# VectorE's order of work inside one attention head: each combination moved up behind its row maximum

## The chip, the cores and the metric

The kernel runs on one core of a Trainium2 chip. The metric is the device time of one launch in microseconds (us); lower is better. A core has five engines with a queue each, which runs in order: TensorE (PE, with its weight loads as PEld), VectorE (DVE), ScalarE (ACT), GpSimd (POOL) and SyncE (SP, which here only issues DMAs). The engines wait for each other on semaphores alone.

## The reference

One step of a streaming encoder layer on 640 tokens (512 of a prompt, 8 streams of 16): a token mixer of two branches, then a mixture of experts, then a final norm. The change touches the token mixer alone. There, per head h of 8:

```
q, k, v, xr, gr = projections of the normed tokens by w_in        # 128 columns each per head
p1, p2 = softmax(q1 k1^T), softmax(q2 k2^T)                        # two maps, chunk-causal for the prompt
attn   = rmsnorm((p1 - lam * p2) @ v)
xc     = conv_b + sum_j xpad[j:j+t] * conv_w[j]                    # causal convolution, width 4
r, i   = sigmoid(xc @ w_ra + b), sigmoid(xc @ w_ri + b)
a      = exp(-8 r softplus(-lambda)); h_t = a_t h_(t-1) + sqrt(1 - a_t^2) (i xc)_t    # recurrence (scan)
y      = h * gelu(gr)
```

The streams attend to 256 cached keys as well.

## The kernel before, in words

The kernel has stages, one `nc.Block()` each. Stage 2 is a loop over heads: head 0 stands by itself, heads 1 to 6 are three turns of a loop of two bodies, head 7 stands by itself. In the profiled execution heads 1 to 6 lie in 128 to 475 us, head 0 before them from about 70 us, and head 7 behind them up to 524 us. Every order in it is written out by hand; nothing is planned by a program. Each engine has its own `body(S)`.

**PE, head h** (L657 on): transposes of the cached keys, the scores of the streams, then this head's projections `xr0`, `xr1` (for the convolution) and `gr0`, `gr1`, and between them the projections of the NEXT head: `kv0` to `kv4` (keys and values of five token tiles), `q0`, `q1`. Among these stand the four prompt tiles qt = 0 to 3 of the attention: `scores(qt)` (L653), `turn_weights(qt)` (transposes of the combined maps, L633), `values(qt)` (L642). Order behind `xr1`: scores 0, kv0, streams' values (L710), kv1, kv2, turn_weights 0, scores 1, gr0, values 0, turn_weights 1, scores 2, gr1, values 1, kv3, turn_weights 2, scores 3, kv4, then the four gate products `ra0 ra1 ri0 ri1` of the recurrence (L735, which wait for `conv_done`), values 2, q0, q1, turn_weights 3, transposes of the keys, values 3. The heads 0 and 7 lack parts: head 0 has no recurrence of a head before to finish on DVE, head 7 has no next head to project.

**The ring of three banks.** All projections and gate products of a head (18 `UNITS`) share three PSUM banks in turn: unit n may start when unit n-3 has been copied out (`S.free`, L424 on). So `gr0` waits for the copy of `kv0`, `ra1` for that of `kv3`, `ri0` for that of `kv4`, and `ri1` for the tanh that reads `ra0`. The copies of kv and xr are on DVE (L891, L922, L932), those of q, gr, the keys and the four tanh (L834) on ACT.

**ACT, head h** (in order): exp 0 of the streams, the tail of the head before (four activations), exp 1, ..., the copies of gr0 and gr1, exp 4, then the four tanh of ra0, ra1, ri0, ri1, then q0, q1. The exponential numbered u = qt+1 (L769) waits for the row maximum of its tile; each is two activations, one per map, with the row sums.

**DVE, head h** is what the change reorders. `prompt_max(S, qt)` masks the scores and takes both maps' row maxima (L867, L860, L861), which releases exp qt+1 on ACT. `combine(S, qt)` waits for that exponential, and forms p1 - lam p2 (L881, L882, L884), which releases `turn_weights(qt)` on PE. `tail_a`, `tail_b`, `tail_c` and `norm_attention` (L443 to L482) finish the recurrence and the norm of head h-1: a reciprocal and products, the scan (L459), the gelu product, the norm. The last of them raises `rnn_done`, for which SP waits before it loads the next head's columns, cached values and the weight tile of gr. `conv` (L895 on) is the convolution, eight instructions, and raises `conv_done`.

**POOL** splits each weight tile of 512 KB into a high and a low part (L167, L170), five tiles per head, when the tile has landed and PE is done with the old one.

Of the kernel before, what the change touches and what calls it, by code (L numbers as in the profile page):

```python
# [88 lines left out]
def build(nc, A, O):  # L89
    top = ExitStack()  # L90
    with top:
# [393 lines left out]
        with nc.Block() as block:  # L485
# [369 lines left out]
            def _(dve):  # L855
# [8 lines left out]
                def prompt_max(S, qt):  # L864
                    n = (qt + 1) * P
                    dve.wait_ge(sc_done, S.h * NQ + (qt + 1))
                    chain(nc.vector.memset(pair[0:64, :, n - 64:n], -BIG))  # L867
                    row_max(S, qt + 1, n)

                def mask_new():  # L870

                    nc.vector.memset(pair[:, :, KNEW:SKEYS], -BIG).then_inc(new_masked, 1)

                def combine(S, qt):

                    u = qt + 1
                    n = (qt + 1) * P
                    dve.wait_ge(exp_done, S.h * 5 + (u + 1))
                    if qt == NQ - 1 and not S.last:
                        mask_new()  # L880
                    chain(nc.vector.reciprocal(stat[:, u, 6:8], stat[:, u, 4:6]))  # L881
                    chain(nc.vector.scalar_tensor_tensor(stat[:, u, 8:9], stat[:, u, 4:5], stat[:, u, 7:8], neglam,  # L882
                                                         ALU.mult, ALU.mult))
                    nc.vector.scalar_tensor_tensor(ebuf[u % 2][:, 0, 0:n], ebuf[u % 2][:, 1, 0:n], stat[:, u, 8:9],  # L884
                                                   ebuf[u % 2][:, 0, 0:n], ALU.mult, ALU.add).then_inc(comb_ready, 1)
# [9 lines left out]
                def conv(S):  # L895

                    cw = hcol[S.par]
                    xcs = xc[:, SEQ:TOK].rearrange("p (b q) -> p b q", q=DS)
                    for j in range(CW):
                        if j == 0:  # L900
                            nc.vector.tensor_scalar(xc[:, 0:SEQ], xpad[:, 0:SEQ], cw[:, R_CW:R_CW + 1],
                                                    cw[:, R_CB:R_CB + 1], ALU.mult, ALU.add)
                            chain(nc.vector.tensor_scalar(xcs, spad[:, :, 0:DS], cw[:, R_CW:R_CW + 1],
                                                          cw[:, R_CB:R_CB + 1], ALU.mult, ALU.add))
                            continue
                        nc.vector.scalar_tensor_tensor(xc[:, 0:SEQ], xpad[:, j:j + SEQ], cw[:, j:j + 1],
                                                       xc[:, 0:SEQ], ALU.mult, ALU.add)
                        ins = nc.vector.scalar_tensor_tensor(xcs, spad[:, :, j:j + DS], cw[:, j:j + 1],
                                                             xcs, ALU.mult, ALU.add)
                        if j < CW - 1:  # L910
                            chain(ins)
                        else:
                            ins.then_inc(conv_done, 1)

                def body(S):
                    h, par = S.h, S.par
                    base = 0 if S.first else h * (BODY_STEPS + TAIL_STEPS) - TAIL_STEPS
                    chain.at(base)
                    dve.wait_ge(ss_done, h + 1)
                    row_max(S, 0, SKEYS)  # L920
                    S.done(dve, "xr0")
                    nc.vector.tensor_copy(xpad[:, 3:3 + HALF], S.bank("xr0")[:, 0:HALF]).then_inc(pr_dve, 1)  # L922

                    dve.wait_ge(exp_done, h * 5 + 1)
                    chain(nc.vector.reciprocal(stat[:, 0, 6:8], stat[:, 0, 4:6]))
                    chain(nc.vector.tensor_scalar(stat[:, 0, 8:10], stat[:, 0, 6:8], msign, None, ALU.mult))
                    for g in range(2):
                        ins = nc.vector.tensor_scalar(selc[:, g, :], cst[:, K_SEL:K_SEL + 64],
                                                      stat[:, 0, 8 + g:9 + g], None, ALU.mult)
                    ins.then_inc(selc_ready, 1)  # L930
                    S.done(dve, "xr1")
                    nc.vector.tensor_copy(xpad[:, 3 + HALF:3 + SEQ], S.bank("xr1")[:, 0:SEQ - HALF])  # L932
                    nc.vector.tensor_copy(spad[:, :, 3:], S.bank("xr1")[:, SEQ - HALF:HALF]
                                          .rearrange("p (b q) -> p b q", q=DS)).then_inc(pr_dve, 1)
                    dve.wait_ge(col_in[par], S.i * 64 + (S.h0 // 2 * 64 + 64))
                    chain(nc.vector.tensor_copy(spad[:, :, 0:3],
                                                hcol[par][:, NCOL:NCOL + 24].rearrange("p (b w) -> p b w", w=3)))
                    prompt_max(S, 0)
                    if not S.first:
                        tail_a(dve, chain, h - 1)  # L940
                    if not S.last:
                        copy_kv(S, 0, 1 - par, h + 1)

                    dve.wait_ge(os_done, h + 1)
                    sample = ons[:, bass.ds(h, 1), :, :].rearrange("p o t c -> p (o t) c")
                    nc.vector.tensor_scalar(sample, bank[7][:, 0:2 * DV].rearrange("p (t c) -> p t c", c=DV),
                                            1.0, None, ALU.mult).then_inc(os_out, 1)
                    combine(S, 0)
                    if not S.last:
                        copy_kv(S, 1, 1 - par, h + 1)  # L950
                        copy_kv(S, 2, 1 - par, h + 1)
                    prompt_max(S, 1)
                    if not S.first:
                        tail_b(chain, h - 1, 1 - par)
                    combine(S, 1)
                    if not S.first:
                        tail_c(dve, chain, h - 1, 1 - par)
                        norm_attention(dve, chain, h - 1)
                    prompt_max(S, 2)
                    conv(S)  # L960
                    combine(S, 2)
                    if not S.last:
                        copy_kv(S, 3, 1 - par, h + 1)
                    prompt_max(S, 3)

                    nc.vector.tensor_scalar(stc[:, bass.ds(h, 1), 0:3], xpad[:, SEQ:SEQ + 3]
                                            .rearrange("p (o c) -> p o c", o=1), 1.0, None, ALU.mult)
                    nc.vector.tensor_scalar(stc[:, bass.ds(h, 1), 3:27].rearrange("p o (b w) -> p (o b) w", w=3),
                                            spad[:, :, DS:DS + 3], 1.0, None, ALU.mult)
                    if not S.last:  # L970
                        copy_kv(S, 4, 1 - par, h + 1)
                    combine(S, 3)

                    S.out(dve, "gr1")
                    chain(nc.vector.tensor_tensor(gw[:, :], gr[par][:, :], gr[par][:, :], ALU.mult))
                    chain(nc.vector.tensor_scalar(gw[:, :], gw[:, :], 0.044715, 1.0, ALU.mult, ALU.add))
                    nc.vector.tensor_tensor(gw[:, :], gw[:, :], gr[par][:, :], ALU.mult).then_inc(gcube, 1)
                    S.out(dve, "ri1")
                    nc.vector.scalar_tensor_tensor(thi[:, :], thi[:, :], 1.0, xc[:, :], ALU.add, ALU.mult)

                    dve.wait_ge(op_done, h + 1)
                    nc.vector.tensor_tensor(oraw[:, :, :], bank[7][:, :].rearrange("p (t c) -> p t c", c=DV),
                                            stat[:, 1:5, 6:7].to_broadcast([P, NQ, DV]), ALU.mult).then_inc(op_out, 1)
                    dve.wait_ge(op_out, h + 1)
                    nc.vector.tensor_tensor(ossq, sample, sample, ALU.mult)
                    chain(nc.vector.tensor_tensor(osq, oraw[:, :, :], oraw[:, :, :], ALU.mult))
                    nc.vector.tensor_reduce(oms[:, NQ:NO], ossq, AX.X, ALU.add)
                    nc.vector.tensor_reduce(oms[:, 0:NQ], osq, AX.X, ALU.add).then_inc(ms_ready, 1)
                    want = BODY_STEPS + (0 if S.first else TAIL_STEPS)
                    assert chain.n == want, (chain.n, want)  # L990
# [984 lines left out]
```

## Time and profile before

| what | value |
|---|---|
| median of 3 runs | 1348.51 us (1347.18 to 1349.4) |
| profiled execution, its own time | 1351.92 us |
| its span | 1350.1 us |
| busy: PE, DVE, ACT, POOL | 85%, 61%, 40%, 38% |
| granted TensorE clock, mean | 0.954 of full |

The span is what the profile covers; the own time is that of the same execution as the runs are timed. A row of the order of time gives an instruction's start, its duration, its engine, line, what it writes and reads, and in brackets how long its engine had been idle and what ended that. Rows that follow each other with the same line are merged with a count.

### The profile page before, as it was taken

What the parts mean: (1) busy time and instruction counts of PE and PEld (TensorE: products, weight loads), DVE (VectorE), ACT (ScalarE), POOL (GpSimd) and SP (SyncE); (2) the same over time, 40 slices, a digit from 0 to 9 for tenths busy, and PEclk for the clock granted to TensorE, in tenths of its full rate; (3) what the DMA queues carried; (4) which work ended last, traced back from release to release, by engine and by line L of the source; (5) the groups of instructions that cost most, each with busy time, mean ns of one, the idle gap of its engine ahead of it and who ended that gap; (6) DMA issues with size and microseconds to landing.
All of it is one profiled execution on the core that took longest, in us unless ns stands there. A gap on an engine that the chain in (4) does not pass through costs nothing. (4 is left out here: it accounts for less than half of the span.)

```text
span 1350.1 us, 20865 instructions
## 1 busy us (share of the span) xinstructions
PE 1152.0 (85%) x7096; PEld 980.4 (73%) x7097; DVE 824.8 (61%) x1204; ACT 542.8 (40%) x873; POOL 510.4 (38%) x267
## 2 busy tenths in 40 slices
PE   2898999899899977999899999577989989888970
PEld 1787888788788866999899845355767767776760
DVE  5436888578588767400512111448788889888765
ACT  3123342333324245111100011126767868777752
POOL 4434161433516102655566300023444444434433
PEclk9999999899999988999899999768999999999995
DMA  4362253232514201422522195024995584799936
GB/s 158 83 165 79 60 142 99 68 105 61 158 52 121 72 1 47 140 78 78 187 78 78 57 337 220 16 88 169 362 336 213 185 297 163 260 361 352 354 143 249
DMA packets 185411, 211.63 MB, mean 157 GB/s; under 512 B 12599, under 2 KB 131383, under 8 KB 185350
## 3 DMA queue, kind: packets, MB, share of 16 engines
q1 hardware_dynamic: 176422, 178.26, 40.6%
q0 software_dynamic: 4608, 16.78, 3.6%
q10 hardware_dynamic: 4320, 15.73, 2.9%
q8 instruction: 43, 0.70, 0.2%
q14 instruction: 18, 0.15, 0.0%
HBM read 184.20 MB, written 26.36 MB: 156 GB/s over the span
## 5 line engine op out<-in xcount | busy, mean ns | idle before, releaser
L1759 ACT ACTIVATE ch<-w 128x1024 fp32r<-128x1024 f32 x240 | 252.0, 1059 | 118.4 <-PE bank L1699 97.0
L1823 DVE TENSOR_TENSOR cl<-w,ch 128x1024 fp32r<-128x1024 f32 x180 | 261.1, 1497 | 41.3 <-ACT ch L1759 37.6
L1669 POOL TENSOR_TENSOR cl<-w,ch 128x1024 fp32r<-128x1024 f32 x60 | 154.2, 2570 | 229.1 <-ACT ch L1759 229.0
L167 POOL TENSOR_TENSOR wh<-raw,zcol 128x1024 fp32r<-128x1024 f32 x40 | 78.7, 1968 | 275.3 <-DMA raw<-in_w_in 194.7
L1697 PE MATMUL bank<-ch,xeh 128*128 128x512 f32 x320 | 132.9, 415 | 45.8 <-DVE cl L1823 42.7
L1698 PE MATMUL bank<-cl,xeh 128*128 128x512 f32 x320 | 127.0, 397 | 0.0
L1699 PE MATMUL bank<-ch,xel 128*128 128x512 f32 x320 | 126.9, 397 | 0.0
L591 PE MATMUL bank<-xh,wh 128*128 128x320 f32 x384 | 122.4, 319 | 0.0
L592 PE MATMUL bank<-xl,wh 128*128 128x320 f32 x384 | 119.2, 310 | 0.0
L593 PE MATMUL bank<-xh,wl 128*128 128x320 f32 x384 | 119.1, 310 | 0.0
L1697 PEld LDWEIGHTS bank<-ch,xeh 128*128 128x128 f32 x320 | 61.3, 192 | 71.8 <-DVE cl L1823 55.3
L170 POOL TENSOR_TENSOR wl<-raw,wh 128x1024 fp32r<-128x1024 f32 x40 | 97.9, 2447 | 3.1
L1117 POOL TENSOR_TENSOR w3h<-wraw,zcol 128x1024 fp32r<-128x1024 f32 x32 | 61.4, 1920 | 87.0 <-PE bank L1160 83.3
L591 PE MATMUL bank<-wh,xh 128*128 128x256 f32 x320 | 93.7, 293 | 0.0
L592 PE MATMUL bank<-wl,xh 128*128 128x256 f32 x320 | 89.9, 281 | 0.0
L593 PE MATMUL bank<-wh,xl 128*128 128x256 f32 x320 | 89.9, 281 | 0.0
L1158 PE MATMUL bank<-bh,w3h 128*128 128x320 f32 x256 | 80.3, 313 | 6.1 <-DVE bl L1240 6.1
L1121 POOL TENSOR_TENSOR w3l<-wraw,w3h 128x1024 fp32r<-128x1024 f32 x32 | 82.0, 2562 | 2.5
L769 ACT ACTIVATE ebuf<-bank,stat 128x384 f32<-128x384 f32 (+3 forms) x80 | 42.3, 534 | 98.8 <-DVE stat L861 98.8
L591 PEld LDWEIGHTS bank<-xh,wh 128*128 128x128 f32 x384 | 72.7, 189 | 10.8 <-issue 8.8
L1159 PE MATMUL bank<-bl,w3h 128*128 128x320 f32 x256 | 80.1, 313 | 0.0
L1160 PE MATMUL bank<-bh,w3l 128*128 128x320 f32 x256 | 80.0, 312 | 0.0
(277 smaller groups left out, 2686.3 us busy)
## 6 DMA issues: line engine op xcount, KB each, us to landing
w<-in_w SPq DMA_DIRECT2D x64, 1024.0 KB, 15.0
w<-in_w SPq DMA_DIRECT2D x16, 2048.0 KB, 10.1
raw<-in_w_in SPq DMA_DIRECT2D x40, 512.0 KB, 4.5
block_outputs<-yb ACTq DMA_DIRECT2D x21, 512.0 KB, 7.2
kc<-in_cache_k SPq DMA_DIRECT2D x8, 1024.0 KB, 6.7
vc<-in_cache_v SPq DMA_DIRECT2D x8, 1024.0 KB, 5.9
wraw<-in_w_in SPq DMA_DIRECT2D x16, 512.0 KB, 3.8
block_outputs<-zero ACTq DMA_DIRECT2D x9, 512.0 KB, 7.1
```

The source lines that it names most:

```text
L170: nc.gpsimd.tensor_tensor(wl[:, :, j, :], r[:, :, :], wh[:, :, j, :].bitcast(F32), ALU.subtract) \
L591: nc.tensor.matmul(out, ah, bh, start=(k == 0), stop=False)
L592: nc.tensor.matmul(out, ah, bl, start=False, stop=False)
L593: mm = nc.tensor.matmul(out, al, bh, start=False, stop=(k == len(pairs) - 1))
L1121: nc.gpsimd.tensor_tensor(w3l[j][:, :, :], wraw[j][:, :, :], w3h[j][:, :, :].bitcast(F32), ALU.subtract).then_inc(w3_split, 1)
L1158: nc.tensor.matmul(out, w3h[j][:, k, :], mh[:, k, c], start=(k == 0), stop=False)
L1669: nc.gpsimd.tensor_tensor(cl[:, c % RING5, :, :], S.raw(c), ch[:, c % RING5, :, :].bitcast(F32), ALU.subtract).then_inc(ch_low_pool, 1)
L1697: nc.tensor.matmul(out, ah, high, start=first, stop=False)
L1698: nc.tensor.matmul(out, ah, low, start=False, stop=False)
L1699: mm = nc.tensor.matmul(out, al, high, start=False, stop=end)
L1759: nc.scalar.activation(ch[:, c % RING5, :, :], S.raw(c), ACT.Copy).then_inc(ch_high, 1)
L1823: nc.vector.tensor_tensor(cl[:, c % RING5, :, :], S.raw(c), ch[:, c % RING5, :, :].bitcast(F32), ALU.subtract).then_inc(ch_low_dve, 1)
```

## The change

It moves three calls in DVE's order and touches nothing else. `combine(S, 0)` goes from behind the copy of the streams' result to directly behind `prompt_max(S, 0)`, ahead of `tail_a`. `combine(S, 1)` goes from between `tail_b` and `tail_c` to directly behind `prompt_max(S, 1)`, ahead of `tail_b`. `combine(S, 2)` goes from behind `conv` to directly behind `prompt_max(S, 2)`, ahead of `conv`. `combine(S, 3)` stays.

```diff
                     prompt_max(S, 0)
+                    combine(S, 0)
                     if not S.first:
                         tail_a(dve, chain, h - 1)
                     if not S.last:
...
                                             1.0, None, ALU.mult).then_inc(os_out, 1)
-                    combine(S, 0)
                     if not S.last:
                         copy_kv(S, 1, 1 - par, h + 1)
                         copy_kv(S, 2, 1 - par, h + 1)
                     prompt_max(S, 1)
+                    combine(S, 1)
                     if not S.first:
                         tail_b(chain, h - 1, 1 - par)
-                    combine(S, 1)
-                    if not S.first:
                         tail_c(dve, chain, h - 1, 1 - par)
                         norm_attention(dve, chain, h - 1)
                     prompt_max(S, 2)
+                    combine(S, 2)
                     conv(S)
-                    combine(S, 2)
                     if not S.last:
                         copy_kv(S, 3, 1 - par, h + 1)
                     prompt_max(S, 3)
```

## Rows read from the trace of the kernel before

**Rows 1.** The page: busy time, share of the span and instructions of each engine.
```profile
PE 1152.0 (85%) x7096; PEld 980.4 (73%) x7097; DVE 824.8 (61%) x1204; ACT 542.8 (40%) x873; POOL 510.4 (38%) x267
```
**Rows 2.** Waits of PE in 250 to 310 us (head 3): total, times, longest.
```profile
PE bank L633 <- DVE ebuf L884: 2.7, 3, 1.1
```
**Rows 3.** Waits of PE in 490 to 550 us (head 7).
```profile
PE bank L633 <- DVE ebuf L884: 9.9, 2, 7.3
...
PE bank L735 <- ACT thr L834: 1.5, 1, 1.5
```
**Rows 4.** DVE in order of time, head 3: start us, us, engine, line.
```profile
262.04 0.48 DVE L445 TENSOR_SCALAR thr<-ra 128x640 f32<-128x640 f32 x1
...
271.73 0.17 DVE L867 MEMSET bank<- 64x128 f32 x1 [0.46 <-PE bank L653]
...
272.73 0.16 DVE L456 TENSOR_TENSOR h0t<-ra,hcol 128x8 f32<-128x8 f32 x1
...
280.46 0.55 DVE L901 TENSOR_SCALAR xc<-xpad,hcol 128x512 f32<-128x512 f32 x1
...
284.06 0.34 DVE L908 SCALAR_TENSOR_TENSOR xc<-spad,hcol,xc 128x128 f32<-128x128 f32 x1
...
287.16 0.17 DVE L867 MEMSET bank<- 64x128 f32 x1 [1.43 <-PE bank L653]
...
290.12 0.42 DVE L891 COPY kvt<-bank 128x256 f32<-128x256 f32 x1 [1.07 <-PE bank L593]
```
**Rows 5.** ACT in order of time, head 3: ends of exp 1 to 4, first tanh.
```profile
262.77 0.20 ACT L769 ACTIVATION_READ_ACCUMULATOR ebuf<-bank,stat 128x1 f32 x1
...
273.68 0.20 ACT L769 ACTIVATION_READ_ACCUMULATOR ebuf<-bank,stat 128x1 f32 x1
...
281.62 0.20 ACT L769 ACTIVATION_READ_ACCUMULATOR ebuf<-bank,stat 128x1 f32 x1
...
290.07 0.20 ACT L769 ACTIVATION_READ_ACCUMULATOR ebuf<-bank,stat 128x1 f32 x1
290.66 1.07 ACT L834 ACTIVATE thr<-bank,hcol 128x320 f32<-128x320 f32 x2 [0.39 <-PE bank L735]
```
**Rows 6.** PE in order of time, head 3: turn_weights 2, and ri1's two passes.
```profile
285.45 0.55 PE L633 MATMUL bank<-cst,ebuf 128*128 128x128 f32 x3 [1.13 <-DVE ebuf L884]
...
291.54 0.70 PE L735 MATMUL bank<-xc,wrg 128*128 128x320 f32 x2
```
**Rows 7.** POOL in order of time, head 3: the split of gr's tile.
```profile
290.42 1.89 POOL L167 TENSOR_TENSOR wh<-raw,zcol 128x1024 fp32r<-128x1024 f32 x1 [28.32 <-DMA raw<-in_w_in]
```
**Rows 8.** DVE in order of time, head 0: inside the convolution.
```profile
103.54 1.98 DVE L908 SCALAR_TENSOR_TENSOR xc<-spad,hcol,xc 128x128 f32<-128x128 f32 x1
105.56 2.81 DVE L906 SCALAR_TENSOR_TENSOR xc<-xpad,hcol,xc 128x512 f32<-128x512 f32 x1
```
**Rows 9.** POOL in order of time, head 0.
```profile
103.41 1.97 POOL L167 TENSOR_TENSOR wh<-raw,zcol 128x1024 fp32r<-128x1024 f32 x1 [17.10 <-PE bank L593]
```
**Rows 10.** ACT in order of time, head 0: the end of exp 3.
```profile
102.15 0.20 ACT L769 ACTIVATION_READ_ACCUMULATOR ebuf<-bank,stat 128x1 f32 x1
```
**Rows 11.** PE in order of time, head 0: turn_weights 2, and ri1.
```profile
109.67 0.63 PE L633 MATMUL bank<-cst,ebuf 128*128 128x128 f32 x3 [3.08 <-DVE ebuf L884]
...
117.31 0.70 PE L735 MATMUL bank<-xc,wrg 128*128 128x320 f32 x2
```
**Rows 12.** Stretch, its length; busy of PE, PEld, DVE, ACT, POOL; clock, DMA, GB/s.
```profile
110.00:112.00 2.00, 2.00 (x7) 0.51 (x4) 0.00 (x0) 0.49 (x1) 0.00 (x0) 0.50 0.00 0
```
**Rows 13.** DVE in order of time, head 7.
```profile
489.68 0.49 DVE L445 TENSOR_SCALAR thr<-ra 128x640 f32<-128x640 f32 x1
...
499.44 0.17 DVE L867 MEMSET bank<- 64x128 f32 x1 [1.79 <-PE bank L653]
...
515.52 0.17 DVE L867 MEMSET bank<- 64x128 f32 x1 [2.96 <-PE bank L653]
```
**Rows 14.** ACT in order of time, head 7: the end of exp 1.
```profile
490.79 0.20 ACT L769 ACTIVATION_READ_ACCUMULATOR ebuf<-bank,stat 128x1 f32 x1
```

## The prediction

> **What bounds the kernel now.** I read the page's busy times first: PE is busy 85% of the span, no other engine over 61% [rows 1], so an edit on DVE is worth what it takes from PE's waits. Then PE's waits by stretch, one per head. In each middle head (1 to 6; head 3 stands for all, and its figures recur within 0.2 us in the other five) PE waits 2.7 us in three places for a combination, before turn_weights 0, 1 and 2 [rows 2]; the third is 1.13 us [rows 6]. In head 0 there is one such wait, 3.08 us [rows 11]. In head 7, where no projections of a next head cover anything, they come to 9.9 us, and 1.5 us more for the tanh that ri1 needs [rows 3]. So 3.1 + 6 x 2.7 + 9.9 = 29 us is all that the edit aims at. Last I read DVE's and ACT's order of time in these heads, to see what DVE does while PE waits, and where DVE itself waits.
>
> **What the change does on DVE.** No instruction is added or removed; what changes is which wait stands in front of what. A combination needs its exponential, and that starts only when the row maximum just ahead has ended. Before, DVE filled this time with tail_a, tail_b or the convolution. Now it stands still for it, three times per head, and everything behind waits too. The waits, from head 3, each from where DVE's next instruction began before to the exponential's end:
> - behind row maximum 0: 262.04 to 262.97 (262.77 + 0.20), 0.93 us [rows 4, 5];
> - behind 1: 272.73 to 273.88, 1.15 us [rows 4, 5];
> - behind 2: 280.46 to 281.82, 1.36 us [rows 4, 5].
>
> Together 3.44 us, and about 0.1 us for three hand-overs that the rows don't resolve: 3.54 us. Against that stands idle time of DVE that vanishes, since it now comes later to where it waited for PE: 0.46 us before row maximum 1 and 1.43 us before row maximum 3 [rows 4]. So row maximum 3, and exp 4 behind it, come 3.54 - 0.46 - 1.43 = 1.65 us later in the head, measured from the end of row maximum 0.
>
> **Middle heads: what PE wins and what is late next.** Combination 0 is ready before PE asks for it. But gr0 behind it needs the ring bank of kv0, whose copy on DVE now comes after combination 0 and tail_a; so of PE's 1.1 us only some 0.3 are won. Combination 1 gains about 0.7. Combination 2 moves ahead of the convolution, 3.94 us (280.46 to 284.40), and behind the three waits, less the 0.46: 3.94 - 3.54 + 0.46 = 0.86 us earlier. Up to kv4, PE is thus about 0.85 us ahead. The convolution ends 3.54 - 0.46 + 1.0 (combination 2 itself, 284.40 to 285.45 with its hand-over, [rows 4, 6]) = 4.1 us later, at 288.5; PE reaches the gate products at about 289.1 (the last two passes of eight before began at 291.54, at 0.27 us each, so the first at 289.9, less 0.85). That still hides it, by 0.6 us.
>
> What is late next is ri1. Its bank is the one that the tanh of ra0 reads, and this tanh stands on ACT behind exp 4. Exp 4 ended at 290.27, and the tanh takes 0.53 (1.07 for two) [rows 5]: 290.27 + 1.65 + 0.53 = 292.45, less 0.1 since the tanh starts into the last read of the row sums (in head 7 PE waited 1.5 us in just this place [rows 3]). ri1 began at 291.54 [rows 6], and now begins at 292.4: **0.85 us later**, although PE was 0.85 us ahead three products before. ri0 needs the copy of kv4 (290.12 before [rows 4]), which goes some 0.5 us later and isn't the last to come. From ri1 on PE runs without a DVE wait to the next head's kv2, so the delay goes whole into the next head. Bounds: 0.85 won, if nothing held ri1, and 1.65 lost, if PE had no slack at all; I take +0.85, the row nearest to it being the wait of rows 3. Six heads: **+5.1 us**.
>
> Cost at nothing: the copy of the streams' result and the copies kv0 to kv2 move by less than PE's distance to their banks but for kv0 above. rnn_done comes 0.93 + 1.15 - 0.46 = 1.6 us later, and with it SP's loads of columns, cached values and gr's tile; that tile is next used by PE half a head later, which hides it. Its split began at 290.42 when the tile landed [rows 7], and will begin near 292.0, while row maximum 3 now ends at 290.4. If the load did not move along, GpSimd's 1.89 us would stand on the row maximum, and each head would lose that much more. Combination 3 is about 1.65 us later, hidden behind the two long products q0 and q1, which PE now starts later as well.
>
> **Head 0.** There is no recurrence of a head before. The 3.08 us go: exp 3 ends at 102.35 [rows 10], combination 2 about 1 us later, and PE is free at 109.67 - 3.08 = 106.59 [rows 11]. The convolution now begins at 103.4, under GpSimd's splits, from 103.41 on [rows 9]. The rows show that two-input instructions stand still beside one: L908 took 1.98 us against 0.34, to 105.52 where GpSimd's 1.97 us ended at 105.38, and L906 2.81 us [rows 4, 8, 9]; without its own 0.55 or so L906 was free at about 107.8. Depending on how many instructions get through before and between the splits, 2.6 to 3.4 us of the convolution are left then: it ends at 110.5 to 111.3. Then the copy of kv3 (0.42 as kv4's [rows 4]), row maximum 3 with exp 4 (287.16 to 290.27, 3.11 us [rows 4, 5]) and the tanh, 0.53: ri1 at 114.5 to 115.4, before 117.31 [rows 11]. So 2.8 to 1.9 us are won; I take **-2.5 us**. The bounds are the whole idle with what the low clock cost behind it (below), -4.6, and -0.7, if the clock falls behind the new waits.
>
> The Trainium skill, "SBUF — State Buffer", section "Who interferes with whom", says that a VectorE instruction with at most one SBUF input, outside the two-port modes, doesn't contend with GpSimd, and that among those which do the first to issue holds the port. By that rule the first two instructions of the convolution run beside the split, and head 0 wins 2.8; if they too stand still, it wins 1.9. No row shows these two beside a split.
>
> **Head 7.** Here DVE sets the pace. The wait behind row maximum 0 is 489.68 to 490.99, 1.31 us [rows 13, 14]; the other two as in head 3, 1.15 and 1.36: 3.82. The idles that vanish are 1.79 and 2.96 us [rows 13], 4.75. So exp 4 and all behind it come 4.75 - 3.82 = 0.93 us earlier: **-0.9 us**. The 9.9 us of PE's waits mostly turn into others, for DVE's work is the same. Bounds -1.5 and 0.
>
> **Sum**: 5.1 - 2.5 - 0.9 = +1.7 us. Against the profiled execution's own 1351.92 that is 1353.6. The median of the runs is 3.4 us lower than that execution; put on the median, 1348.5 + 1.7 = 1350.2 us. A measurement can tell about 0.2% here, 2.7 us; +1.7 lies within.
>
> **Rivals.**
> - *A, slower: the clock falls in the new gap.* In the middle heads PE will idle some 0.9 us before ri0 and 0.75 before ri1, close together. After 3.08 us of idle in head 0 the granted clock was 0.50, its lower level of 1.2 GHz [rows 12], and turn_weights 2 to ri1 took 7.64 us (109.67 to 117.31) where head 3 took 6.09 (285.45 to 291.54) [rows 6, 11]: 1.55 us per fall. It decides once about one head is hit. In three of six: +1.7 + 4.65 = +6.4, 1354.9. For it: work between the gaps is thin. Against: the three waits of before, up to 1.13 us, cost no clock. 17%.
> - *B, faster: ri1 isn't held.* If the tanh had more slack than I read, PE would keep its 0.85 us per head: -5.1 - 2.5 - 0.9 = -8.5, 1340.0. For it: PE does wait for the combinations, and these are earlier. Against: the ring, and the wait in head 7. 12%.
> - *C, slower: all of DVE's delay reaches PE*, 1.65 per head: 9.9 - 3.4 = +6.5, 1355.0. Against: ri1 had slack, as no wait is recorded in head 3. 5%.
> - *D, nothing moves*: PE's gains and losses are both covered, 1348.5. 10%.
>
> **How the numbers follow.** My forecast has 56%; its own range is 1348.5 to 1352.2, and a fifth of it lies over +2.7. Same: 45 + 10 = 55%. Slower: 11 + 17 + 5 = 33%. Faster: B, 12%. The range for 8 in 10 takes in A and C to 1356, and goes down to 1346, leaving B out.
>
> **What would show it.** In a middle head: no idle before turn_weights 0, gr0 led by the copy of kv0; DVE idle three times, 0.9 to 1.4 us, for ACT; PE idle before L735 for the tanh, near 0.75 us; the head's period 0.85 us longer. In head 0 the wait of 3.08 gone and the convolution slow under the splits; in head 7 an idle near 1.4 before turn_weights 0 in place of 7.3, and another of 5 before turn_weights 1. I am wrong if PE has no wait at L735 in heads 1 to 6 (then B), or if a head there has a clock under 1.00 behind it (A).

## The result, and the profile after

| | before | after |
|---|---|---|
| median of 5 runs | 1348.82 us (1347.18 to 1350.74) | 1356.36 us (1355.20 to 1357.17) |
| profiled execution, its own time | 1351.92 us | 1355.53 us |
| its span | 1350.1 us | 1353.7 us |
| granted TensorE clock, mean | 0.954 | 0.958 |

The change makes the kernel slower: the ratio is 1.0054 (1.0039 to 1.0069), and a repeat on another chip gave 1.0047 (1.0032 to 1.0061). Forecast were 1350.2 us and most likely no measurable difference; the time also lies 0.36 us above the range. The two profiled executions differ by 3.6 us, the medians by 7.5 (5.3 to 9.3 by the ratio; the repeat's 4.3 to 8.2); both numbers are followed below.

The busy line of the page, against [rows 1]: every engine does what it did.
```profile
PE 1153.5 (85%) x7096; PEld 976.9 (72%) x7097; DVE 823.7 (61%) x1204; ACT 540.4 (40%) x873; POOL 510.1 (38%) x267
```
PE's waits in 250 to 310 us (head 3), against [rows 2]: total, times, longest.
```profile
PE bank L591 <- DVE kvt L891: 1.0, 1, 1.0
PE bank L633 <- DVE ebuf L884: 1.0, 1, 1.0
PE bank L735 <- DVE kvt L891: 0.8, 1, 0.8
PE bank L735 <- ACT thr L834: 0.5, 1, 0.5
```
Three waits of 2.7 us for combinations have become one of 1.0 for a combination (the third) and three new ones: gr0 for the copy of kv0, ri0 for the copy of kv4, ri1 for the tanh. All four come to 3.3 us. So PE waits more, for things further back in DVE's queue, while the combinations that it had waited for are ready.

DVE's own waits in the same stretch have a new row: DVE stands still for ACT, three times.
```profile
DVE stat L881 <- ACT ebuf L769: 3.3, 3, 1.3
```
DVE in order of time, head 3, against [rows 4]: the three new waits (L881), the row maxima 1 and 3 without an idle before them (L867) and the copy of kv4 (L891).
```profile
262.67 0.17 DVE L881 RECIPROCAL stat<-stat 128x2 f32<-128x2 f32 x1 [0.87 <-ACT ebuf L769]
...
271.93 0.17 DVE L867 MEMSET bank<- 64x128 f32 x1
...
274.11 0.17 DVE L881 RECIPROCAL stat<-stat 128x2 f32<-128x2 f32 x1 [1.09 <-ACT ebuf L769]
...
283.20 0.17 DVE L881 RECIPROCAL stat<-stat 128x2 f32<-128x2 f32 x1 [1.30 <-ACT ebuf L769]
...
288.49 0.17 DVE L867 MEMSET bank<- 64x128 f32 x1
...
290.31 0.43 DVE L891 COPY kvt<-bank 128x256 f32<-128x256 f32 x1
```
ACT, the end of exp 4 and the tanh, against [rows 5]; then PE, the third combination and the gate products, against [rows 6].
```profile
291.40 0.20 ACT L769 ACTIVATION_READ_ACCUMULATOR ebuf<-bank,stat 128x1 f32 x1
291.49 0.94 ACT L834 ACTIVATE thr<-bank,hcol 128x320 f32<-128x320 f32 x2
```
```profile
284.33 0.55 PE L633 MATMUL bank<-cst,ebuf 128*128 128x128 f32 x3 [0.95 <-DVE ebuf L884]
...
288.80 1.24 PE L735 MATMUL bank<-xc,wrg 128*128 128x320 f32 x4
290.79 0.81 PE L735 MATMUL bank<-xc,wrg 128*128 128x320 f32 x2 [0.75 <-DVE kvt L891]
292.07 0.81 PE L735 MATMUL bank<-xc,wrg 128*128 128x320 f32 x2 [0.47 <-ACT thr L834]
```
What a head costs is read from one row that recurs, the last transpose at the head's end. Before and after, heads 3 and 4:
```profile
301.05 0.33 PE L617 MATMUL bank<-cst,kvt 128*128 128x128 f32 x1 [0.22 <-ACT qT L787]
357.43 0.33 PE L617 MATMUL bank<-cst,kvt 128*128 128x128 f32 x1 [0.22 <-ACT qT L787]
```
```profile
301.68 0.33 PE L617 MATMUL bank<-cst,kvt 128*128 128x128 f32 x1 [0.22 <-ACT qT L787]
359.06 0.33 PE L617 MATMUL bank<-cst,kvt 128*128 128x128 f32 x1 [0.22 <-ACT qT L787]
```
The period is 56.38 us before and 57.38 after. The same row, and the first transpose of stage 3 (526.33 before, 529.49 after), split the whole difference. "Again" is the profiled execution of the repeat.

| stretch | predicted | after | again |
|---|---|---|---|
| up to head 0's first projections' end (70.26 to 71.37) | 0 | +1.1 | +1.1 |
| head 0 | -2.5 | -2.2 | -2.2 |
| the four middle heads without a turn of the loop | +3.4 | +3.9 | +3.9 |
| the two with one (before 61.4 and 60.3 us, after 61.2 and 61.7, again 62.9 and 61.6) | +1.7 | +1.1 | +2.7 |
| head 7 | -0.9 | -0.8 | 0.0 |
| stages behind | 0 | +0.4 | -0.1 |
| sum: span against 1350.1 | +1.7 | +3.6 | +5.5 |

The fourth row needs the clock beside it. At each turn of the loop PE idles 2.8 to 2.9 us in all three traces, and the granted clock is 0.50 around it, for 3.4 or for 6.8 us. Stretch 242 to 254 us of before, after and again (head 3, the first of the two), with the clock in the third column from the end:
```profile
242.00:254.00 12.00, 9.52 (x73) 7.67 (x74) 5.32 (x7) 4.80 (x10) 6.84 (x4) 0.72 0.50 145
```
```profile
242.00:254.00 12.00, 8.85 (x77) 7.35 (x77) 6.54 (x8) 5.13 (x11) 8.17 (x4) 0.86 0.54 155
```
```profile
242.00:254.00 12.00, 8.79 (x66) 6.54 (x65) 6.46 (x7) 4.22 (x9) 8.17 (x4) 0.72 0.44 128
```
So the first trace of after has 3.4 us less of the low clock there, and its head 3 is 1.6 us shorter than again's (61.24 against 62.88). In head 5 the clock is alike in all three (0.86 in 358 to 370 us), and so are after and again (61.67 and 61.62). Compared at like clock the two heads cost +2.7 us, and the first trace flatters the change by 1.6: its +3.6 would be about +5.2 by this estimate, near the repeat's +5.5.

### The profile page after: what moved, and what is told of

Its sections match the earlier page's. It is cut to its first block and busy times, and to the rows that moved or that the text cites. A ratio compares the mean times of both kernels' runs of the same rounds, so it can differ in the third digit from the quotient of the medians.

```text
span 1353.7 us, 20865 instructions
## 1 busy us (share of the span) xinstructions
PE 1153.5 (85%) x7096; PEld 976.9 (72%) x7097; DVE 823.7 (61%) x1204; ACT 540.4 (40%) x873; POOL 510.1 (38%) x267
## 5 line engine op out<-in xcount | busy, mean ns | idle before, releaser
L591 PE MATMUL bank<-xh,wh 128*128 128x320 f32 x384 | 122.4, 319 | 6.0 <-DVE kvt L891 6.0
L1116 POOL TENSOR_TENSOR w3h<-wraw,zcol 128x1024 fp32r<-128x1024 f32 x32 | 61.4, 1919 | 86.6 <-PE bank L1159 83.0
L591 PE MATMUL bank<-wh,xh 128*128 128x256 f32 x320 | 93.8, 293 | 0.0
L591 PEld LDWEIGHTS bank<-xh,wh 128*128 128x128 f32 x384 | 72.7, 189 | 17.3 <-issue 8.8
```

Source lines behind the costliest of these rows:

```text
L591: nc.tensor.matmul(out, ah, bh, start=(k == 0), stop=False)
```

## The experiments

Each is compared with the kernel before, timed beside it on the same chip. Where a difference is given "by the ratios", it is that of the two ratios to before; the ratio is not the quotient of the two medians. T is the theory of the prediction: the one thing that costs is DVE standing still behind a row maximum, and it is to be followed through the ring to PE; the rivals are those of the prediction, or named in the expectation.

**The changed kernel again.** No edit.

> The changed kernel once more, for a second time and a second trace. Theory T (order): in each middle head (1 to 6) PE loses about 0.97 us, because gr0 waits for the copy of kv0, ri0 for that of kv4 and ri1 for the tanh of ra0 behind exp 4; with -2.2 in head 0 and -0.8 in head 7 that is +2.8 us, always the same, and whatever the time is above +2.8 is TensorE's clock, which the trace would show below 1.00 at another place. Rival R (clock in the new gaps): the measured +7.5 comes from half-clock stretches behind the idle before the gate products in some heads, which the first trace happened not to have; this trace then shows one or more in heads 1 to 6. Time by T alone 1351.6, by R 1354 to 1359.

1356.88 us against 1351.13, ratio 1.0047 (1.0032 to 1.0061). No middle head has a granted clock under 1.00 between two turns of the loop: rival A isn't what happened. T put the time at 1351.6 and missed it by 5 us. The rival R of this expectation had the number (1354 to 1359), but the low clock that it wants behind the gate products isn't in this trace either. From 128 to 478 us PE's waits are, after and then before:
```profile
PE bank L591 <- DVE kvt L891: 6.0, 6, 1.0
PE bank L633 <- DVE ebuf L884: 5.7, 6, 1.0
...
PE bank L735 <- DVE kvt L891: 4.5, 6, 0.8
PE bank L735 <- ACT thr L834: 2.8, 6, 0.5
```
```profile
PE bank L633 <- DVE ebuf L884: 16.1, 18, 1.1
```
Each of the four stands in all six heads.

**The three moves one at a time.** Each is the kernel before with one combination moved.

```diff
# combination 0 alone
                 prompt_max(S, 0)
+                combine(S, 0)
...
-                combine(S, 0)
# combination 1 alone
                 prompt_max(S, 1)
+                combine(S, 1)
                 if not S.first:
                     tail_b(chain, h - 1, 1 - par)
-                combine(S, 1)
# combination 2 alone
                 prompt_max(S, 2)
+                combine(S, 2)
                 conv(S)
-                combine(S, 2)
```

> Of the change only combination 0 moved. T: DVE waits 0.9 us for exp 1 and gives back 0.46 before row maximum 1, so combinations 1 and 2 and all behind come 0.5 us later: +0.5 in each of 6 heads, 0 in head 0, about -0.5 in head 7: +2.5 us. R2 (a wait in DVE's order costs nothing while PE has projections left): PE's 1.1 us before turn_weights 0 is won in each head, -6 us.

> Of the change only combination 1 moved. T: it comes 1.1 us earlier, of which PE can use 0.5; but DVE waits 1.15 us for exp 2 with nothing to give it back before combination 2, for which PE already waits: combination 2, row maximum 3 and ri1 come 1.2 us later, +1.2 in each of 6 heads, +1.2 in head 7, 0 in head 0: +8.3 us, more than the whole change. R2: PE's 0.5 us is won, -3 us.

> Of the change only combination 2 moved ahead of the convolution. T: it is ready 2.5 us earlier, PE's 1.1 us before turn_weights 2 is gone; DVE's wait for exp 3, 1.36 us, is paid by the 1.43 us that it idled before row maximum 3, so exp 4 keeps its place and ri1 comes 0.7 to 0.8 us earlier: -0.8 x 6, -2.2 in head 0, -1.7 in head 7: -8.5 us, faster than both kernels. R3 (the wait for exp 3 goes on to the convolution and so to the gate products): ri1 comes 1 us later, +4 us.

Measured: combination 0 alone 1353.72 us, ratio 1.0020 (1.0010 to 1.0031); 1 alone 1370.94, 1.0158 (1.0142 to 1.0174); 2 alone 1342.04, 0.9945 (0.9930 to 0.9961). Before was 1351.13 in all three. The period of a clean middle head (56.39 before, 57.37 after) is 56.92, 57.52 (in the one head with a full clock) and 55.68.

So the first and the last are as T has them (the last is 9.1 us faster by the medians, 7.4 by the ratio), and the change is made of one good move and two bad ones. The good one is the one whose wait is bought with 3.94 us of advance: DVE stands still 1.30 us (1.36 forecast) and the combination jumps over the whole convolution. The other two wait 0.9 and 1.1 us for an advance that PE had not much use for.

Combination 1 alone cost 19.8 us where T gave 8.3, and most of the excess is rival A's mechanism, in another kernel than the one it was made for. The rows of PE's order of time at 169 us (head 1) with the passes behind, and the window (stretch, its length; busy of PE, PEld, DVE, ACT, POOL; clock, DMA, GB/s):
```profile
168.86 0.90 PE L633 MATMUL bank<-cst,ebuf 128*128 128x128 f32 x3 [2.99 <-DVE ebuf L884]
169.69 2.08 PE L653 MATMUL bank<-kT,qT 64*128 64x512 f32 x4
...
172.08 0.41 PE L592 MATMUL bank<-wl,xh 128*128 128x256 f32 x1
```
```profile
169.00:174.00 5.00, 5.00 (x17) 3.17 (x18) 2.19 (x4) 0.49 (x1) 0.67 (x1) 0.50 0.80 197
```
Combination 1 comes earlier and lets PE through; combination 2 stays behind the convolution and comes later. In head 3 the waits before turn_weights 0, 1 and 2 were 1.11, 0.48 and 1.13 us; they are 1.11, none and 3.00 now. Behind this idle of 3 us the granted clock is 0.50, its lower level of 1.2 GHz: the scores of tile 3 take 2.08 us (1.13 at the full clock), a pass of kv4 0.41 (0.28). It happened in five of the six middle heads; in the sixth, head 6, the same idle of 2.98 us had no lower clock behind it (1.00 in 477 to 484 us). In the full change, which has the move of combination 2 as well, this idle isn't there (0.95 us before turn_weights 2). Of three moves one alone can thus be worse than all together: 2.6 + 19.8 - 9.1 = 13.3 us added up, 5.8 measured together (1356.88 - 1351.13).

**Before again.** No edit, as a floor for the others.

> The kernel before, once more, for its own ratio to itself and a second trace. Both theories: ratio 1.000 within 0.15%. T (order): stage 2 has the same waits, head for head; where its time differs from the first trace, TensorE's half-clock stretches differ in number or length. If the gap between the traces (+3.6) and the timings (+6 to +7.5) of the changed kernel is chance of these stretches, this trace ends 1 to 3 us earlier than the first one.

1350.16 us against 1350.44, ratio 0.9998 (0.9988 to 1.0008). Its profiled execution has the span of the first, 1350.1 us, and lies 1.7 us above the median of its own runs. The expectation's case, that the second trace ends 1 to 3 us earlier because the first had happened on more of the low clock, didn't come: the low clock at the two turns is that of the first trace. It was the first trace of after that had less of it.

**Two of PE's new waits, each taken away in the changed kernel.** The first puts the copy of kv0 ahead of combination 0. The second moves exp 4 on ACT behind the tanh of ra0 and ra1, so that ri1's bank is not held by it.

```diff
# DVE, kv0 first
                 prompt_max(S, 0)
+                if not S.last:
+                    copy_kv(S, 0, 1 - par, h + 1)
                 combine(S, 0)
...
-                if not S.last:
-                    copy_kv(S, 0, 1 - par, h + 1)
# ACT, tanh first: exp 4 into the loop over ra0, ra1, ri0, ri1
-                softmax_exp(S, 4, 4 * P)
...
+                    if name == "ri0":
+                        softmax_exp(S, 4, 4 * P)
```

> The changed kernel with the copy of kv0 put ahead of combination 0, into DVE's wait for exp 1. T: gr0 no longer waits for it (PE's 1.0 us per head gone there), and DVE's 0.42 us of copy lies inside a wait that is paid anyway, so combinations 1 and 2, exp 4 and ri1 come 0.4 us earlier: 2.5 us less than the changed kernel over six heads, still 3 to 4 over the kernel before. R2 (PE's wait for kv0 is what the change costs): all of its 1.0 us per head comes back, -6 us, level with before.

> The changed kernel with ACT's tanh of ra0 and ra1 ahead of exp 4 instead of behind it. T: ri1's bank comes free before PE asks; left is ri0's wait for the copy of kv4, so ri1 starts 0.5 to 0.7 us earlier in each middle head: -3 to -4 us against the changed kernel, some +2 to +3 over the kernel before; the waits of L735 for thr vanish. R4 (all behind row maximum 3 is late anyway, exp 4 above all): no change, or slower by the 1.1 us that exp 4 now waits.

The copy of kv0 first: 1354.62 us, ratio to before 1.0029 (1.0017 to 1.0042), by the ratios 2.4 us less than the repeat of the change. PE's wait for the ring's bank at L591 is gone, and most of it (0.81 us) is back in front of combination 1 (the period is 56.96, 0.41 less, not 1.0; T's 2.5 us over six heads came out, R2's 6 did not): PE's wait in 250 to 310 us, where after had 1.0.
```profile
PE bank L633 <- DVE ebuf L884: 1.8, 2, 1.0
```
The tanh first: 1350.52 us, ratio to before 0.9997 (0.9987 to 1.0007), 6.8 us less than the repeat of the change; the period is 56.62, 0.75 less, which makes 4.5 us over six heads; head 0 is 0.9 us shorter as well (53.45 against 54.33). T had forecast 3 to 4 us back and a time 2 to 3 us over before, so it had the sign and fell short of the size; R4's "no change, or slower" is out. The row for the tanh has gone and nothing has come in its place:
```profile
PE bank L591 <- DVE kvt L892: 1.1, 1, 1.1
...
PE bank L735 <- DVE kvt L892: 0.7, 1, 0.7
```
So the last wait in the head, ri1 behind exp 4, was what carried most of DVE's delay into the next head (0.75 of 0.98 us), as the prediction had it. More came back than the recorded 0.47 us.

**Both together in the changed kernel** (the two diffs above).

> The changed kernel with both single repairs: the copy of kv0 ahead of combination 0, and ACT's tanh of ra0 and ra1 ahead of exp 4. T (order): the two add up in a middle head, since one shortens what comes before row maximum 3 (0.41 us) and the other what comes after (0.75 us): period 0.2 us under that of the kernel before, and with head 0 -3 to -4 us against it. R4 (both repairs remove the same wait): no better than the tanh alone, level with before.

1351.84 us, ratio to before 1.0015 (1.0001 to 1.0028), periods 56.34 to 56.50 in the four clean heads: 0.2 us under that of the tanh alone, level with before, but the time is over both. In head 3 PE now waits for combination 1 as well as 2 (L633, 1.8 us in two waits), and 0.7 for the copy of kv4. The two don't add up, and T's -3 to -4 us is missed; R4's "level with before" is nearer. That the time is even 2 us over that of the tanh alone (by the ratios) doesn't show in the trace, whose span is the shorter one (1348.6 against 1349.0 us). The executions of this kernel lie far apart, 1348.4 to 1358.2 us, the traced one at 1350.4, and the three slowest have the lowest granted clock (0.949 to 0.951, the others 0.953 to 0.955). What lowers it in them, and not in those of the tanh alone, stays open, as none of them was traced.

**Only what T calls good.** Combination 2 moved; combination 0 inside tail_a, behind its reciprocal of 4.15 us, so that the exponential is covered; tanh first.

```diff
# in tail_a, behind the reciprocal of L446
+                combine(S, 0)
# behind the copy of the streams' result
-                combine(S, 0)
+                if S.first:
+                    combine(S, 0)
...
                 prompt_max(S, 2)
+                combine(S, 2)
                 conv(S)
-                combine(S, 2)
```

> The kernel before with combination 2 ahead of the convolution, combination 0 inside tail_a behind its reciprocal (heads 1 to 7; exp 1 is long done there, so DVE waits for nothing), and the tanh of ra0 and ra1 ahead of exp 4. T: against combination 2 alone (-8.7) PE wins up to 0.46 us per head at combination 0 (DVE's idle before row maximum 1 is what can go, its work sets the rest) and 0.4 at ri1: -5 us more, -13 to -14 against the kernel before. R4: exp 4, now behind two tanh, holds combination 3 and turn_weights 3, and nothing is won beyond -9.

1340.55 us, ratio 0.9934 (0.9914 to 0.9953): faster than both kernels, but 3 to 5 us short of T. The interval overlaps with that of combination 2 alone, and R4's "nothing beyond -9" fits the time; it doesn't fit the heads, of which the undisturbed ones are 1.1 us shorter (54.6 against 55.7). In heads 2, 4 and 6 PE waited for something new, the selection matrix that DVE scales for the streams (L931 by this kernel's lines). In head 4 this scaling took 2.06 us under a split of GpSimd that began at 306.39, where it takes 0.42 in the kernel before; PE waited 2.26 us, and the clock behind it was 0.50:
```profile
308.48 1.94 PE L695 MATMUL bank<-selc,ebuf 128*128 128x64 f32 x10 [2.26 <-DVE selc L931]
...
309.00:313.00 4.00, 4.00 (x21) 3.66 (x20) 2.98 (x6) 2.55 (x6) 1.73 (x1) 0.50 0.01 4
```
Head 4 took 59.3 us, the best of the others 54.6, and this is most of what T is short of in this trace. The other executions lie between 1335.7 and 1347.7 us, the four slowest with the lowest granted clock (0.947 to 0.950).

**Row maximum 0 out from under GpSimd's split.** In each middle head the two-element scaling behind row maximum 0 takes 1.62 us beside a split, where it takes 0.17 elsewhere. The row maxima of the streams and of the tiles 0 to 2 were written to PSUM, so that the scaling reads no SBUF, and the copy of the history columns (1.60 us beside a split) was put ahead of the wait for xr1 (not shown below). In the kernel before, in c2_only, and in c2_only with tanh first.

```diff
-                    chain(nc.vector.tensor_reduce(stat[:, u, 0:2], pair[:, :, 0:n], AX.X, ALU.max))
+                    row = pair[:, 0, 508:510] if n < 512 else stat[:, u, 0:2]
+                    chain(nc.vector.tensor_reduce(row, pair[:, :, 0:n], AX.X, ALU.max))
-                    nc.vector.tensor_scalar(stat[:, u, 2:4], stat[:, u, 0:2], -SCALE, None, ALU.mult) \
+                    nc.vector.tensor_scalar(stat[:, u, 2:4], row, -SCALE, None, ALU.mult) \
```

> The kernel before, with none of the moved combinations, and two DVE instructions kept from standing still beside GpSimd's weight split: the copy of the convolution's history (24 elements) is made before xr1 is waited for, and the row maxima of all tiles but the last go through a free corner of their PSUM bank, so that the scaling by -1/8 reads PSUM. T: both were on DVE's path to combination 0 (1.6 us each against 0.17), so in middle heads DVE is 2 us earlier there; PE's 1.1 us before turn_weights 0 go, the rest is held by scores 1: -1.1 a head, -7 us. R5 (the scaling still stands still with its source in PSUM): unchanged.

> Combination 2 ahead of the convolution alone, with the two instructions kept clear of GpSimd as in the run before it. T: the gains add, since PE's waits before turn_weights 0 and 2 are two different ones; period of a middle head 2.0 us under before, head 0 and 7 as with combination 2 alone: -15 us. R5: -9 as combination 2 alone.

> As the run before it, and the tanh of ra0 and ra1 ahead of exp 4. T: ri1 no longer waits, 0.2 to 0.4 us per middle head more, -16 to -17 us against before; and no wait of PE for the selection matrix (L693) in any head, which the run called best had in three heads, once 2.3 us with half clock behind it. R4: exp 4 behind two tanh makes combination 3 late and takes this back, -14.

Measured: 1349.69 us, ratio 0.9990 (0.9981 to 1.0000); 1342.21, 0.9934 (0.9921 to 0.9947); 1340.41, 0.9924 (0.9909 to 0.9940). None is what T had: not the 7 us of the first, not the 15 of the second (R5's 9 fits), not the 16 to 17 of the third, nor R4's 14. PE still waits 1.15 us before turn_weights 0 in head 3 of the first, and the order of time shows why. DVE before, then DVE and POOL with the edit, at the start of head 3's row maximum 0 (L445 took 0.48 us before, [rows 4]):
```profile
260.50 1.62 DVE L861 TENSOR_SCALAR stat<-stat 128x2 f32<-128x2 f32 x1
```
```profile
259.94 0.16 DVE L862 TENSOR_SCALAR stat<-bank 128x2 f32<-128x2 f32 x1
260.02 2.36 DVE L445 TENSOR_SCALAR thr<-ra 128x640 f32<-128x640 f32 x1
...
259.62 2.41 POOL L170 TENSOR_TENSOR wl<-raw,wh 128x1024 fp32r<-128x1024 f32 x1
```
The scaling was freed (0.16), and the next instruction with SBUF on both sides stood still in its place until the split's end. Here freeing the first instruction that met the split only put the next one in its place. The last of the three has the lowest ratio of the study, 10 us under before, but its interval overlaps with those of the second and of the kernel in the section above. It, too, waits for the selection matrix (2.4, 0.4 and 0.3 us in heads 2, 4, 6); behind the 2.4 the clock stayed at 1.00:
```profile
194.94 1.55 PE L693 MATMUL bank<-selc,ebuf 128*128 128x64 f32 x12 [2.41 <-DVE selc L930]
...
196.00:202.00 6.00, 6.00 (x86) 5.47 (x86) 5.76 (x8) 2.64 (x7) 1.03 (x1) 1.00 0.01 4
```

## Why the prediction was wrong, point by point

**In short.** The mechanism in a head was right, its size nearly so. What failed are two steps of the sum: taking 3.4 us off the profiled execution to get to the median, where after's median lies 0.8 us above its profiled execution; and putting at nothing what lies outside a head's order, where 1.1 us stood at the start of stage 2 and 1.0 us in the two heads with a turn of the loop beyond their 0.85 each. The points in order:

**The mechanism was right.** DVE's three waits in head 3 came to 3.3 us (0.87, 1.09, 1.30; forecast 0.93, 1.15, 1.36). The idle before the row maxima 1 and 3 went (1.89 us, [rows 4]). The row maximum 3 came 1.57 us later in the head (forecast 1.65), the tanh behind exp 4 held ri1, and the delay went on into the next head. The moves of combination 0 and of combination 2 alone, and the copy of kv0 put first, came out as the same working has them. Combination 1 alone did but for the clock (its one head at full clock grew by 1.13 us, 1.2 forecast), and the tanh first had the sign and not the size. The runs that put repairs together all fell short of it.

**Middle heads: +0.85 forecast, +0.98 measured**, so +5.9 for six instead of +5.1, had all been like the clean ones. Measured from the end of row maximum 0 (262.04 before, 262.67 - 0.87 = 261.80 after), the first gate product stands at 27.9 us before and 27.0 after, 0.9 early as forecast; ri1 at 29.5 and 30.3, 0.77 late, forecast 0.85. The rest of the period, 0.2 us, lies between ri1 and the next row maximum and wasn't in the sum. I had said that the copy of kv4 isn't the last to come at ri0, and that was wrong: it came 0.75 us after PE, and ri1 only had 0.47 left to wait. The sum doesn't change by it, since ri1 sets the end.

A recorded wait is also smaller than what it costs. Four passes of gate products stand 0.27 apart, so ri0 would have begun at 288.80 + 4 x 0.27 = 289.88; it began at 290.79, 0.9 us late with 0.75 recorded. ri1 would have been 0.54 behind it, at 291.33, and began at 292.07: 0.74 late with 0.47 recorded. The record counts from the end of the last pass, but passes overlap. With 2.9 us more of waits over the six heads (19.0 against 16.1), the periods grew by 5.1.

**Head 0: -2.5 forecast, -2.2 measured.** DVE, then POOL, at its convolution, against [rows 8, 9]:
```profile
104.49 2.21 DVE L901 TENSOR_SCALAR xc<-xpad,hcol 128x512 f32<-128x512 f32 x1
106.62 2.40 DVE L903 TENSOR_SCALAR xc<-spad,hcol 128x128 f32<-128x128 f32 x1
```
```profile
104.52 1.89 POOL L167 TENSOR_TENSOR wh<-raw,zcol 128x1024 fp32r<-128x1024 f32 x1 [17.10 <-PE bank L593]
106.49 2.44 POOL L170 TENSOR_TENSOR wl<-raw,wh 128x1024 fp32r<-128x1024 f32 x1
```
Both one-input instructions stood still under the two halves of the split (0.54 and 0.34 us without one), so the case of 1.9 us was the nearer. The Trainium skill, "SBUF — State Buffer", section "Who interferes with whom", leaves an instruction with one SBUF input out of the contention unless it is in a two-port mode; these rows agree only if these two were in such a mode. The same section names tensor_scalar, which both are, among those that can enter one; I passed over this when I let the two run beside the split. The idle of 3.08 us and the clock of 0.50 behind it ([rows 11, 12]) went; at 110 to 112 us the clock is 1.00 now:
```profile
110.00:112.00 2.00, 2.00 (x19) 1.92 (x17) 1.93 (x5) 0.00 (x0) 0.00 (x0) 1.00 0.00 0
```

**Head 7: -0.9 forecast, -0.8 and 0.0 measured.** PE's waits, 493 to 526 us:
```profile
PE bank L633 <- DVE ebuf L884: 4.8, 3, 2.6
PE bank L642 <- DVE ons L947: 2.6, 1, 2.6
PE bank L735 <- DVE xc L908: 2.3, 1, 2.3
```
The wait of 7.27 us before turn_weights 0 has gone, and the one before turn_weights 1 is 2.59 where I had said 5: the other half comes one step earlier, as values 0 waits for the copy of the streams' result (L947), which frees its bank. I had followed the ring of three but not this bank. Behind the wait for the convolution the clock was 0.50 in both traces of the changed kernel, for 3.4 us in the first (0.76 over 518.6 to 525.6 us) and for twice as long in the repeat (0.51 over the same stretch). There the eight gate products took 4.98 us, and the gain was lost:
```profile
520.37 4.98 PE L735 MATMUL bank<-xc,wrg 128*128 128x320 f32 x8 [2.25 <-DVE xc L908]
```

**What wasn't in the sum.** The first 70 us run the same instructions, yet head 0 begins 1.1 us later. The last section shows the place: TensorE's clock rises 2.4 us later. Over the 14 traces kept here, whose instructions up to this point are the same, head 0 begins between 70.15 and 71.62 us. The kernels with combination 0 alone and combination 2 alone are among the late ones (71.6), combination 1 alone is among the early ones (70.3), so it doesn't follow the edit. What decides it stays open. The two heads with a turn of the loop gave +1.1 in one and +2.7 us in the other execution of the changed kernel; the granted clock beside the table accounts for the difference. At like clock they cost 1.0 us more than the 0.85 each that I gave them, and for that I have no row.

**From the execution to the median.** Against its own execution the forecast was 1353.6 and the measured 1355.53 us. I then took off 3.4 us for the median, as if the profiled execution of after would also lie above its runs. It lies 0.8 us under their median, in the repeat 0.6 above, while that of before lies 3.1 and, in its repeat, 1.7 above. So of the miss of 6.2 us (1356.36 - 1350.2) 1.9 lie in the sum (1.1 at the start, 0.8 in the rest of the table), and 4.2 in this step, the largest single error. It could not be seen from one execution; its price is the spread of single executions about their median, which the range should have held: over all kernels here the profiled execution lies from 1.6 us under to 3.1 over the median of its runs. Part of the 4.2 is the clock: the profiled execution of after has the highest granted clock of its five (0.958; the others 0.952 to 0.956), and with the 1.6 us of head 3 counted as above, the traces say +5.2 and +5.5. That is the lower end of the first interval of the timings (5.3 to 9.3 us) and within the second (4.3 to 8.2). The remaining distance to the medians' 7.5 no trace here explains, and it may be chance.

**The chances.** I gave 33% to slower, with my own case at +1.7 us and a bound of 2.7 for what can be told apart. The unknowns of the sum (the start, the turns of the loop, the median) are as large as this distance, and all fell on the same side. The size of a head was forecast well; that the time ended 0.36 us outside the range, and not inside, is chance.

## What to carry to other kernels

A step moved directly behind what releases its input isn't free on an engine that works in order: the engine now stands through the other engine's latency. Weigh, step by step, the wait that it takes on (here 0.9, 1.1, 1.3 us) against the distance that the step jumps and against what PE waits for; only the move that jumped a long block ahead of a real wait paid (7 to 9 us), the other two cost. Where several waits of one engine are spread out, don't gather them into one: waits of 1.1, 0.5 and 1.1 us had no lower clock behind them, one idle of 3 us had in five heads of six.

## What the runs showed of the hardware

- **A clock column of 1.00 can mean that the profile has no record of the clock.** At the start of stage 2, PE begins its projections at the same moment (46.44 and 46.47 us). Stretch 48.5 to 50.9 us, before and then after, and one pass of after in it:
```profile
48.50:50.90 2.40, 2.40 (x22) 2.40 (x21) 0.00 (x0) 0.00 (x0) 1.63 (x1) 1.00 0.82 239
```
```profile
48.50:50.90 2.40, 2.40 (x14) 2.40 (x13) 0.00 (x0) 0.00 (x0) 1.65 (x1) 1.00 0.88 243
...
50.46 0.41 PE L591 MATMUL bank<-wh,xh 128*128 128x256 f32 x1
```
The column reads 1.00 in both, PE is busy throughout in both, yet 14 instructions fall into it instead of 22, and a pass takes the 0.41 us that it takes at a granted 0.50 (172.08 above). Before, the slow passes end at 48.7 us, after at 51.1: this is the 1.1 us. The clock's records explain the column. In the trace of before the first one begins at 48.6 us, in that of after at 51.0, each where the passes turn fast; earlier there is none, and the column shows 1.00 for want of one. In one trace of the study, combination 2 alone, the records begin earlier, at 40.6 us, and there the same slow passes (12 in 2.2 us) stand beside the lower level:
```profile
48.50:50.70 2.20, 2.20 (x12) 2.20 (x12) 0.00 (x0) 0.00 (x0) 2.20 (x1) 0.50 0.59 174
```
Compare the number or duration of equal passes, not the column alone.
- **An idle of two to three us may or may not have the low clock behind it.** Waits up to 1.3 us before turn_weights never had it in a middle head between two turns of the loop. Idles of 2.97 to 3.00 us in combination 1 alone had it in five heads and not in the sixth (2.98); of the two waits for the selection matrix the one of 2.26 us had it, the one of 2.41, in another kernel, had not. So the length of the idle alone doesn't settle it here.
- **Beside GpSimd's split a VectorE scaling or copy from SBUF to SBUF stands still, however small**: a scaling of two elements took 1.62 us instead of 0.17, while one from PSUM took 0.16. Not every instruction does: in the kernel before a reciprocal of two elements, in SBUF on both sides, ran in 0.15 us within the split that began at 290.42 [rows 7], and the two-input instruction behind it stood still.
```profile
290.78 0.15 DVE L881 RECIPROCAL stat<-stat 128x2 f32<-128x2 f32 x1
290.96 1.36 DVE L882 SCALAR_TENSOR_TENSOR stat<-stat,lam 128x1 f32<-128x1 f32 x1
```
